# Summing the two up blocks of a seven-product unit with an accumulating DMA instead of a GpSimd subtraction

## The chip, the core and the metric

The kernel runs on one core of a Trainium2 chip. The metric is the device time of one launch in microseconds (us); the lower the better. Engines are called as in the profile: PE (TensorE matmul), PEld (its weight loads), DVE (VectorE), ACT (ScalarE), POOL (GpSimd), SP (SyncE, which issues the weight loads from HBM).

## The reference

One decoder layer over 256 tokens with a model width of 2048 in float32: a mixer (mLSTM and retention heads with one input and one output projection) and then a SwiGLU feed-forward network of width 5632, each between RMS norms. The change touches only the feed-forward part:

```
h = rmsnorm(x, g_ffn_pre)
ff = (silu(h @ w_gate) * (h @ w_up)) @ w_down
x = x + rmsnorm(ff, g_ffn_post)
```

## The kernel before

Every float32 weight is split into a rounded part and a rest (`w_hi` by ACT, `w_lo` by DVE as raw minus `w_hi`), so that a product is three fast matmuls. The weights arrive in `raw`, four chunks of 128 x 2048, loaded by SP's queue up to four units ahead; `w_hi` and `w_lo` have four slots each (AHEAD), and ACT may fill a slot only when PE has finished the piece that used it last.

A **unit** of the feed-forward part is two blocks of 128 weight rows by two blocks of 512 columns: for gate and up one block column of `w_up` and one of `w_gate`; for the down product two block columns of `w_down`. A plain unit (R) has two pieces, up and gate. A **seven-product unit** (S) computes the 2x2 block product with seven block products in place of eight, as Strassen and Winograd do, in four pieces, 0 to 3. A group of gate and up (512 columns, nine of them with the plan RRSRSRSR, then one RRSRSRRR) has its S units at n = 2, 4, 6, called the first, second and third unit below. The two halves of the down product have five S units each. That makes 29 + 10 = 39 S units.

In a unit's chunk the four blocks stand side by side: b12 and b22 (the up half), b11 and b21 (the gate half). Around the products three engines work on them:

- POOL, **T3** (L613): b12 becomes b22 - b12, as soon as the up half has arrived. In the down product five small token sums (L637 to L645) follow here.
- ACT hi0 and DVE lo0 round piece 0 (blocks b22 and b11). Then DVE, **T2** (L1559): b11 becomes b12 + b11. It waits for its own lo0 and for T3.
- ACT hi1 and DVE lo1 round piece 1 (b21).
- POOL, **T1** (L617): b22 becomes b22 - b11, after T2. POOL, **T4** (L619): b21 becomes b21 - b11, after lo1.
- ACT hi2 and DVE lo2 round piece 2 (b12 and b11; hi2 waits for T3 and T2). ACT hi3 and DVE lo3 round piece 3 (b22 and b21; hi3 waits for T1 and T4).

The hi's of S pieces are L983, of R pieces L972; the lo's are L1553 and L1550. Each engine executes its list in order. On DVE the order is lo0, T2, lo1, lo2, lo3, then the two lo's of the next R unit, then the next unit's lo0. On POOL it is T3 of a unit, T1, T4, then T3 of the next unit. PE waits for the lo of each piece (L1681 holds all its matmuls). SP reloads a chunk when the last lo that reads it is done.

The POOL part before, of which one unit is:

```
pool.wait_ge(raw_up[q], up_arrived(i, n))
pool.tensor_tensor(b12, b22, b12, ALU.subtract).then_inc(t3_ready, 1)
if between:
    between()
pool.wait_ge(t2_ready, made + 1)
pool.tensor_tensor(b22, b22, b11, ALU.subtract).then_inc(t14_ready, 1)
pool.wait_ge(lo_done, ff_base(i) + (plan.base[n] + 2))
pool.tensor_tensor(b21, b21, b11, ALU.subtract).then_inc(t14_ready, 1)
```

POOL's own queue carries four DMAs before the change: `neg_rows` (L591) and `neg_all` (L593) early, and the two post-norm gains (L606, L628), the last of them right ahead of the first T3 of the down product.

Of the kernel before, what the change touches and what calls it, by code (L numbers as in the profile page):

```python
# [24 lines left out]
ALU = mybir.AluOpType  # L25
# [28 lines left out]
FF_GROUPS = D_FF // 512  # L54
# [152 lines left out]
def hybrid_layer(nc, x, positions, g_mix_pre, w_in, conv_w, conv_b, b_igate, b_fgate, g_mlstm_head,  # L207
                 g_ret_head, w_out, g_mix_post, g_ffn_pre, w_gate, w_up, w_down, g_ffn_post,
                 inv_freq, out):
    with ExitStack() as ctx:  # L210
# [157 lines left out]
        s_ready = sem("s_ready")  # L368
        t3_ready = sem("t3_ready")
        t2_ready = sem("t2_ready")  # L370
        t14_ready = sem("t14_ready")
        p1_out = sem("p1_out")
        part_step = sem("part_step")
        part_done = sem("part_done")
# [195 lines left out]
        def _(pool):  # L570
# [37 lines left out]
            def weight_sums(i, n, plan, between=None):  # L608

                q, made = chunk_of(i, n), sums_index(i, n)  # L610
                b12, b22, b11, b21 = (raw[:, q, 512 * c:512 * (c + 1)] for c in range(4))
                pool.wait_ge(raw_up[q], up_arrived(i, n))
                pool.tensor_tensor(b12, b22, b12, ALU.subtract).then_inc(t3_ready, 1)  # L613
                if between:
                    between()
                pool.wait_ge(t2_ready, made + 1)
                pool.tensor_tensor(b22, b22, b11, ALU.subtract).then_inc(t14_ready, 1)  # L617
                pool.wait_ge(lo_done, ff_base(i) + (plan.base[n] + 2))
                pool.tensor_tensor(b21, b21, b11, ALU.subtract).then_inc(t14_ready, 1)  # L619

            with pool.Fori(1, FF_GROUPS - 1) as i:
                for n in SEVEN:
                    weight_sums(i, n, FULL)
            for n in SEVEN[:2]:
# [5 lines left out]
            def token_sums(d, n):  # L630

                a11, a21 = d_whole[:, 0, 0:P], d_whole[:, 0, P:SEQ]
                a12, a22 = d_whole[:, 1, 0:P], d_whole[:, 1, P:SEQ]
                if d:
                    pool.wait_ge(d_step, 5 * d)
                    pool.wait_ge(d_ready, d)
                pool.tensor_tensor(d_whole[:], ffT[:, 2 * n:2 * n + 2, 0:SEQ].bitcast(F32),  # L637
                                   ffT[:, 2 * n:2 * n + 2, SEQ:2 * SEQ].bitcast(F32), ALU.add).then_inc(d_step, 1)
                pool.wait_ge(d_step, 5 * d + 1)
                pool.tensor_tensor(d_sum[:, 0], a21, a22, ALU.add).then_inc(d_step, 1)  # L640
                pool.tensor_tensor(d_sum[:, 2], a11, a21, ALU.subtract).then_inc(d_step, 1)
                pool.wait_ge(d_step, 5 * d + 2)
                pool.tensor_tensor(d_sum[:, 1], d_sum[:, 0], a11, ALU.subtract).then_inc(d_step, 1)
                pool.wait_ge(d_step, 5 * d + 4)
                pool.tensor_tensor(d_sum[:, 3], a12, d_sum[:, 1], ALU.subtract).then_inc(d_step, 1)  # L645

# [8 lines left out]
        def _(act):  # L655
# [306 lines left out]
            def unit_hi(i, odd, plan, m):  # L962
# [12 lines left out]
                if piece == 0:  # L975
                    act.wait_ge(raw_up[q], arrived)
                    act.wait_ge(raw_full[q], arrived + 16 * (R_FF + 2))
                elif piece == 2:
                    act.wait_ge(t3_ready, sums_index(i, n) + 1)
                    act.wait_ge(t2_ready, sums_index(i, n) + 1)  # L980
                elif piece == 3:
                    act.wait_ge(t14_ready, 2 * sums_index(i, n) + 2)
                act.activation(slot_blocks(w_hi, slot, piece), seven_blocks(piece, q),  # L983
                               ACT.Copy).then_inc(hi_done, 1)

# [75 lines left out]
        def _(dve):  # L1061
# [426 lines left out]
            def up_sums(i, plan, c0, subs=None):  # L1488

                dve.wait_ge(part_done, 2 * i)  # L1490
                dve.wait_ge(sub_done, ff_base(i) + (subs or plan.subs - 1))
                for t in range(TT):
                    dve.tensor_tensor(ff(t, i), ff(t, i), bank[:, c0 + 2 + t, :], ALU.add).then_inc(up_sum, 1)

            def gate_sum_of(i, t, c0):

# [26 lines left out]
            def seven_sums(j):  # L1523

                k = 2 * SEVEN[j]
                whole = s_whole[:, j]
                a11, a21 = whole[:, 0, 0:P], whole[:, 0, P:SEQ]
                a12, a22 = whole[:, 1, 0:P], whole[:, 1, P:SEQ]
                link(dve.tensor_tensor(whole, h2T[:, k:k + 2, 0:SEQ].bitcast(F32),
                                       h2T[:, k:k + 2, SEQ:2 * SEQ].bitcast(F32), ALU.add))  # L1530
                link(dve.tensor_tensor(s_sum[:, j, 0], a21, a22, ALU.add))
                link(dve.tensor_tensor(s_sum[:, j, 1], s_sum[:, j, 0], a11, ALU.subtract))
                link(dve.tensor_tensor(s_sum[:, j, 2], a11, a21, ALU.subtract))
                dve.tensor_tensor(s_sum[:, j, 3], a12, s_sum[:, j, 1], ALU.subtract).then_inc(s_summed, 1)

# [8 lines left out]
            def unit_lo(i, odd, plan, m):  # L1544
# [10 lines left out]
                   .then_inc(lo_done, 1)  # L1555
                if piece == 0:
                    dve.wait_ge(lo_done, ff_base(i) + (m + 1))
                    dve.wait_ge(t3_ready, sums_index(i, n) + 1)
                    dve.tensor_tensor(raw[:, q, 1024:1536], raw[:, q, 0:512], raw[:, q, 1024:1536], ALU.add)\  # L1559
                       .then_inc(t2_ready, 1)  # L1560

            def partial_sums(i, plan, s0):
# [2 lines left out]
                p7, p5, p6 = bank[:, s0, :], bank[:, s0 + 1, :], bank[:, s0 + 3, :]  # L1565
                dve.wait_ge(sub_done, ff_base(i) + plan.after_seven)
                dve.wait_ge(p1_out, i)
                dve.tensor_tensor(u4, p1, p6, ALU.add).then_inc(part_step, 1)
                dve.wait_ge(part_step, 2 * i - 1)
                dve.tensor_tensor(u3, u4, p7, ALU.add).then_inc(part_step, 1)  # L1570
                dve.wait_ge(part_step, 2 * i)
# [526 lines left out]
```

## Time and profile before

| | |
|---|---|
| median of 3 runs | 1212.13 us (1212.02 to 1212.75) |
| profiled execution, its time | 1212.14 us |
| profiled execution, its span | 1210.4 us |
| mean granted TensorE clock | 0.998 of full speed (2.4 GHz) |
| busy: PE, PEld, DVE, ACT, POOL | 1193.8, 997.9, 926.5, 673.1, 265.7 us |
| DMA | 230.67 MB, 191 GB/s over the span |

The span runs from the first to the last instruction; the run's own time is 1.7 us more. The feed-forward groups with S units lie from about 520 us of the span on, the down product from 964 us to the end. A row of the timeline gives the start, the length, the engine, the line, the operation and its output and inputs; the bracket at its end is the idle time of that engine just before, and who ended it. A row with x2 or more merges instructions that follow on each other.

### The profile page before, as it was taken

The page shows a single profiled execution, that of the slowest core. Times are in us where ns is not written, and L with a number is a line of the kernel's source. Part 1 is how long each engine was busy: PE and PEld are TensorE (multiplying, and loading weights), DVE is VectorE, ACT ScalarE, POOL GpSimd, SP SyncE. Part 2 cuts the span into 40 slices and gives each one's busy share as a digit, 9 for nine tenths or more (in the row PEclk, how much of TensorE's full clock was granted, in tenths as well). Part 3 has the DMA queues.
Part 4 walks back from the last instruction along what each step waited for, and adds up shares of the span by engine and source line. Part 5 has one row for each costly group of instructions (what it writes and reads, how often), then busy time and mean ns, then how long its engine had stood idle before and what let it go on. Part 6 is the DMA issues. An engine that isn't in the chain of part 4 may idle for free.

```text
span 1210.4 us, 16331 instructions
## 1 busy us (share of the span) xinstructions
PE 1193.8 (99%) x5766; PEld 997.9 (82%) x5766; DVE 926.5 (77%) x1162; ACT 673.1 (56%) x890; POOL 265.7 (22%) x202
## 2 busy tenths in 40 slices
PE   8999999999999999999999999999999999999997
PEld 7888888888888888888888888888888878887885
DVE  6657777877777655777887888788888788669866
ACT  5654766474654645656555555555656555445543
POOL 1000200000000000004333323432332287227710
PEclk9999999999999999999999999999999999999999
DMA  8656868768686556454565556566555745764562
GB/s 312 206 154 159 230 168 174 170 135 219 161 198 194 194 189 199 158 199 154 195 209 208 190 187 214 172 208 208 196 188 188 255 156 199 243 193 158 188 225 70
DMA packets 122723, 230.67 MB, mean 191 GB/s; under 512 B 8104, under 2 KB 24752, under 8 KB 122032
## 3 DMA queue, kind: packets, MB, share of 16 engines
q1 hardware_dynamic: 122208, 226.85, 60.4%
q0 software_dynamic: 464, 3.15, 0.6%
q8 instruction: 30, 0.49, 0.2%
q14 instruction: 21, 0.17, 0.0%
HBM read 227.88 MB, written 2.11 MB: 190 GB/s over the span
## 4 chain that ended last, share of the span: by engine, by line
PE 93%; DVE 3%; ACT 2%; DMA 1%; issue 0%; SPq 0%; DVEq 0%; ACTq 0%
PE bank L1681 92%; DMA resid<-in_x 1%; PE bank L1958 1%; DVE w_lo L1553 1%; DVE w_lo L1074 0%; ACT w_hi L668 0%; PE bank L1686 0%; PE bank L1875 0%; DVE ff_out L1618 0%; ACT decay L778 0%; ACT w_hi L983 0%; ACT L824 0%; DVE w_lo L1550 0%; DVE h L1101 0%; DVE gT L1288 0%
## 5 line engine op out<-in xcount | busy, mean ns | idle before, releaser
L1681 PE MATMUL bank<-w_hi,h2T 128*128 128x512 f32 x1126 | 359.2, 390 | 0.0
L1074 DVE TENSOR_TENSOR w_lo<-raw,w_hi 128x1024 fp32r<-128x1024 f32 x172 | 209.3, 1222 | 127.6 <-ACT w_hi L668 126.9
L668 ACT ACTIVATE w_hi<-raw 128x1024 fp32r<-128x1024 f32 x172 | 180.9, 1058 | 174.3 <-PE bank L1681 155.1
L1681 PE MATMUL bank<-hT,w_hi 128*128 128x512 f32 x768 | 270.5, 396 | 0.0
L1553 DVE TENSOR_TENSOR w_lo<-raw,w_hi 128x1024 fp32r<-128x1024 f32 (+1 forms) x156 | 206.1, 1326 | 71.6 <-ACT w_hi L983 71.5
L1681 PEld LDWEIGHTS bank<-w_hi,h2T 128*128 128x128 f32 x1126 | 211.4, 188 | 44.0
L1550 DVE TENSOR_TENSOR w_lo<-raw,w_hi 128x1024 fp32r<-128x1024 f32 x170 | 213.3, 1287 | 34.7 <-ACT w_hi L972 34.1
L983 ACT ACTIVATE w_hi<-raw 128x1024 fp32r<-128x1024 f32 (+1 forms) x156 | 148.6, 954 | 159.7 <-PE bank L1681 133.1
L972 ACT ACTIVATE w_hi<-raw 128x1024 fp32r<-128x1024 f32 x170 | 174.6, 1055 | 89.1 <-PE bank L1681 88.8
L1681 PE MATMUL bank<-hT,w_lo 128*128 128x256 f32 x768 | 214.6, 279 | 0.0
L1681 PE MATMUL bank<-w_lo,h2T 128*128 128x512 f32 x543 | 211.3, 389 | 0.0
L1681 PE MATMUL bank<-w_hi,ffT 128*128 128x512 f32 x604 | 190.3, 390 | 0.3 <-DVE w_lo L1550 0.3
L1681 PEld LDWEIGHTS bank<-hT,w_hi 128*128 128x128 f32 x768 | 143.9, 187 | 31.6
L1681 PEld LDWEIGHTS bank<-hT,w_lo 128*128 128x128 f32 x768 | 145.0, 189 | 0.0
L1681 PEld LDWEIGHTS bank<-w_hi,ffT 128*128 128x128 f32 x604 | 113.4, 188 | 25.7 <-DVE w_lo L1550 2.1
L1681 PEld LDWEIGHTS bank<-w_lo,h2T 128*128 128x128 f32 x543 | 102.0, 188 | 21.0
L617 POOL TENSOR_TENSOR raw<-raw 128x512 f32<-128x512 f32 x39 | 62.2, 1595 | 252.4 <-DVE raw L1559 252.4
L1681 PE MATMUL bank<-w_lo,ffT 128*128 128x512 f32 x302 | 117.6, 389 | 0.0
L613 POOL TENSOR_TENSOR raw<-raw 128x512 f32<-128x512 f32 x39 | 63.6, 1630 | 226.7 <-DMA raw<-in_w_up 190.7
L1681 PE MATMUL bank<-w_hi,hT 128*128 128x512 f32 x256 | 81.3, 393 | 1.6 <-DVE w_lo L1074 1.6
L1681 PE MATMUL bank<-w_hi,mixT 128*128 128x512 f32 x256 | 80.1, 391 | 0.0
L1681 PEld LDWEIGHTS bank<-w_lo,ffT 128*128 128x128 f32 x302 | 56.7, 188 | 11.4
(232 smaller groups left out, 1300.7 us busy)
## 6 DMA issues: line engine op xcount, KB each, us to landing
raw<-in_w_in SPq DMA_DIRECT2D x63, 1024.0 KB, 10.5
raw<-in_w_down SPq DMA_DIRECT2D x88, 512.0 KB, 5.0
raw<-in_w_up SPq DMA_DIRECT2D x80, 512.0 KB, 4.0
raw<-in_w_gate SPq DMA_DIRECT2D x80, 512.0 KB, 4.9
raw<-in_w_out SPq DMA_DIRECT2D x16, 1024.0 KB, 5.0
raw<-in_w_gate SPq DMA_DIRECT2D x4, 1024.0 KB, 5.3
raw<-in_w_up SPq DMA_DIRECT2D x4, 1024.0 KB, 6.0
resid<-in_x SPq DMA_DIRECT2D x2, 1024.0 KB, 7.3
```

Source lines behind the costliest of these rows:

```text
L613: pool.tensor_tensor(b12, b22, b12, ALU.subtract).then_inc(t3_ready, 1)
L617: pool.tensor_tensor(b22, b22, b11, ALU.subtract).then_inc(t14_ready, 1)
L668: act.activation(part_of(w_hi, rnd, s), src, ACT.Copy).then_inc(hi_done, 1)
L972: act.activation(w_hi[:, slot, :], raw[:, q, SUB * piece:SUB * (piece + 1)], ACT.Copy).then_inc(hi_done, 1)
L983: act.activation(slot_blocks(w_hi, slot, piece), seven_blocks(piece, q), ACT.Copy).then_inc(hi_done, 1)
L1074: dve.tensor_tensor(part_of(w_lo, rnd, s), raw_sub(rnd, s)[1], part_of(w_hi, rnd, s).bitcast(F32), ALU.subtract).then_inc(lo_done, 1)
L1550: dve.tensor_tensor(w_lo[:, slot, :], raw[:, q, SUB * piece:SUB * (piece + 1)], w_hi[:, slot, :].bitcast(F32), ALU.subtract).then_inc(lo_d ...
L1553: dve.tensor_tensor(slot_blocks(w_lo, slot, piece), seven_blocks(piece, q), slot_blocks(w_hi, slot, piece).bitcast(F32), ALU.subtract)\
L1681: return pe.matmul(out_, lhsT, rhs, start=start, stop=stop, skip_group_check=True)
L1958: ins = pe.transpose(bank[:, b0 + j // 2, c:c + P], ff(t)[:, j * P:(j + 1) * P], ident)
```

## The change

T3 becomes a DMA that POOL issues and that adds b22 onto b12 in place; its semaphore goes up by 16 when the data has landed. As this is a sum and not a difference, signs turn: the token sums, T1 and T4, the product sums on DVE (same number of operations, of the same shapes). On POOL T4 now comes ahead of T1, and both stand behind the wait for lo1; T1 and T4 have a semaphore each. hi2 no longer waits for T3. POOL's loop over the groups is written out instead of run as a loop.

```diff
--- before.py
+++ after.py
@@ -368,7 +368,8 @@
         s_ready = sem("s_ready")
         t3_ready = sem("t3_ready")
         t2_ready = sem("t2_ready")
-        t14_ready = sem("t14_ready")
+        t1_ready = sem("t1_ready")
+        t4_ready = sem("t4_ready")
         p1_out = sem("p1_out")
         part_step = sem("part_step")
         part_done = sem("part_done")
@@ -610,15 +611,15 @@
                 q, made = chunk_of(i, n), sums_index(i, n)
                 b12, b22, b11, b21 = (raw[:, q, 512 * c:512 * (c + 1)] for c in range(4))
                 pool.wait_ge(raw_up[q], up_arrived(i, n))
-                pool.tensor_tensor(b12, b22, b12, ALU.subtract).then_inc(t3_ready, 1)
+                pool.dma_start(b12, b22, accum_op=ALU.add).then_inc(t3_ready, 16)
                 if between:
                     between()
+                pool.wait_ge(lo_done, ff_base(i) + (plan.base[n] + 2))
                 pool.wait_ge(t2_ready, made + 1)
-                pool.tensor_tensor(b22, b22, b11, ALU.subtract).then_inc(t14_ready, 1)
-                pool.wait_ge(lo_done, ff_base(i) + (plan.base[n] + 2))
-                pool.tensor_tensor(b21, b21, b11, ALU.subtract).then_inc(t14_ready, 1)
-
-            with pool.Fori(1, FF_GROUPS - 1) as i:
+                pool.tensor_tensor(b21, b21, b11, ALU.add).then_inc(t4_ready, 1)
+                pool.tensor_tensor(b22, b11, b22, ALU.subtract).then_inc(t1_ready, 1)
+
+            for i in range(1, FF_GROUPS - 1):
                 for n in SEVEN:
                     weight_sums(i, n, FULL)
             for n in SEVEN[:2]:
@@ -637,10 +638,10 @@
                 pool.tensor_tensor(d_whole[:], ffT[:, 2 * n:2 * n + 2, 0:SEQ].bitcast(F32),
                                    ffT[:, 2 * n:2 * n + 2, SEQ:2 * SEQ].bitcast(F32), ALU.add).then_inc(d_step, 1)
                 pool.wait_ge(d_step, 5 * d + 1)
-                pool.tensor_tensor(d_sum[:, 0], a21, a22, ALU.add).then_inc(d_step, 1)
+                pool.tensor_tensor(d_sum[:, 0], a22, a21, ALU.subtract).then_inc(d_step, 1)
                 pool.tensor_tensor(d_sum[:, 2], a11, a21, ALU.subtract).then_inc(d_step, 1)
                 pool.wait_ge(d_step, 5 * d + 2)
-                pool.tensor_tensor(d_sum[:, 1], d_sum[:, 0], a11, ALU.subtract).then_inc(d_step, 1)
+                pool.tensor_tensor(d_sum[:, 1], d_sum[:, 0], a11, ALU.add).then_inc(d_step, 1)
                 pool.wait_ge(d_step, 5 * d + 4)
                 pool.tensor_tensor(d_sum[:, 3], a12, d_sum[:, 1], ALU.subtract).then_inc(d_step, 1)
 
@@ -976,10 +977,10 @@
                     act.wait_ge(raw_up[q], arrived)
                     act.wait_ge(raw_full[q], arrived + 16 * (R_FF + 2))
                 elif piece == 2:
-                    act.wait_ge(t3_ready, sums_index(i, n) + 1)
                     act.wait_ge(t2_ready, sums_index(i, n) + 1)
                 elif piece == 3:
-                    act.wait_ge(t14_ready, 2 * sums_index(i, n) + 2)
+                    act.wait_ge(t1_ready, sums_index(i, n) + 1)
+                    act.wait_ge(t4_ready, sums_index(i, n) + 1)
                 act.activation(slot_blocks(w_hi, slot, piece), seven_blocks(piece, q),
                                ACT.Copy).then_inc(hi_done, 1)
 
@@ -1490,7 +1491,7 @@
                 dve.wait_ge(part_done, 2 * i)
                 dve.wait_ge(sub_done, ff_base(i) + (subs or plan.subs - 1))
                 for t in range(TT):
-                    dve.tensor_tensor(ff(t, i), ff(t, i), bank[:, c0 + 2 + t, :], ALU.add).then_inc(up_sum, 1)
+                    dve.tensor_tensor(ff(t, i), bank[:, c0 + 2 + t, :], ff(t, i), ALU.subtract).then_inc(up_sum, 1)
 
             def gate_sum_of(i, t, c0):
 
@@ -1528,8 +1529,8 @@
                 a12, a22 = whole[:, 1, 0:P], whole[:, 1, P:SEQ]
                 link(dve.tensor_tensor(whole, h2T[:, k:k + 2, 0:SEQ].bitcast(F32),
                                        h2T[:, k:k + 2, SEQ:2 * SEQ].bitcast(F32), ALU.add))
-                link(dve.tensor_tensor(s_sum[:, j, 0], a21, a22, ALU.add))
-                link(dve.tensor_tensor(s_sum[:, j, 1], s_sum[:, j, 0], a11, ALU.subtract))
+                link(dve.tensor_tensor(s_sum[:, j, 0], a22, a21, ALU.subtract))
+                link(dve.tensor_tensor(s_sum[:, j, 1], s_sum[:, j, 0], a11, ALU.add))
                 link(dve.tensor_tensor(s_sum[:, j, 2], a11, a21, ALU.subtract))
                 dve.tensor_tensor(s_sum[:, j, 3], a12, s_sum[:, j, 1], ALU.subtract).then_inc(s_summed, 1)
 
@@ -1555,7 +1556,7 @@
                    .then_inc(lo_done, 1)
                 if piece == 0:
                     dve.wait_ge(lo_done, ff_base(i) + (m + 1))
-                    dve.wait_ge(t3_ready, sums_index(i, n) + 1)
+                    dve.wait_ge(t3_ready, 16 * sums_index(i, n) + 16)
                     dve.tensor_tensor(raw[:, q, 1024:1536], raw[:, q, 0:512], raw[:, q, 1024:1536], ALU.add)\
                        .then_inc(t2_ready, 1)
 
@@ -1565,7 +1566,7 @@
                 p7, p5, p6 = bank[:, s0, :], bank[:, s0 + 1, :], bank[:, s0 + 3, :]
                 dve.wait_ge(sub_done, ff_base(i) + plan.after_seven)
                 dve.wait_ge(p1_out, i)
-                dve.tensor_tensor(u4, p1, p6, ALU.add).then_inc(part_step, 1)
+                dve.tensor_tensor(u4, p1, p6, ALU.subtract).then_inc(part_step, 1)
                 dve.wait_ge(part_step, 2 * i - 1)
                 dve.tensor_tensor(u3, u4, p7, ALU.add).then_inc(part_step, 1)
                 dve.wait_ge(part_step, 2 * i)
```

## Rows read from the trace of the kernel before

**Rows 1.** The page, chain that ended last: shares of the span by engine

```profile
PE 93%; DVE 3%; ACT 2%; DMA 1%; issue 0%; SPq 0%; DVEq 0%; ACTq 0%
```

**Rows 2.** Windows over the down product: length, then busy time of each engine

```profile
964.00:1073.00 109.00, 107.87 (x477) 87.76 (x476) 82.65 (x67) 57.01 (x62) 57.89 (x41) 1.00 0.61 207
1073.00:1180.00 107.00, 105.55 (x462) 85.73 (x461) 86.36 (x72) 55.34 (x64) 56.62 (x40) 1.00 0.56 190
```

**Rows 3.** Timeline, PE and PEld: first and last third-unit wait, and the longest

```profile
572.06 0.19 PEld L1681 LDWEIGHTS bank<-w_hi,s_third 128*128 128x128 f32 x1 [0.27 <-DVE w_lo L1553]
...
913.62 0.19 PEld L1681 LDWEIGHTS bank<-w_hi,s_third 128*128 128x128 f32 x1 [0.30 <-DVE w_lo L1553]
...
1098.69 0.50 PE L1681 MATMUL bank<-w_hi,d_ops 128*128 128x512 f32 x1 [1.16 <-DVE w_lo L1553]
```

**Rows 4.** Waits, the whole span: total us, times, longest

```profile
ACT w_hi L983 <- POOL raw L619: 25.4, 10, 2.6
```

**Rows 5.** Timeline of POOL, second and third unit of one gate/up group

```profile
718.62 1.29 POOL L613 TENSOR_TENSOR raw<-raw 128x512 f32<-128x512 f32 x1
726.42 1.68 POOL L617 TENSOR_TENSOR raw<-raw 128x512 f32<-128x512 f32 x1 [6.51 <-DVE raw L1559]
728.06 1.29 POOL L619 TENSOR_TENSOR raw<-raw 128x512 f32<-128x512 f32 x1
729.30 2.28 POOL L613 TENSOR_TENSOR raw<-raw 128x512 f32<-128x512 f32 x1
...
738.51 2.27 POOL L619 TENSOR_TENSOR raw<-raw 128x512 f32<-128x512 f32 x1
```

**Rows 6.** Timeline of DVE, the same stretch

```profile
718.94 3.19 DVE L1553 TENSOR_TENSOR w_lo<-raw,w_hi 128x1024 fp32r<-128x1024 f32 x2
722.05 2.35 DVE L1550 TENSOR_TENSOR w_lo<-raw,w_hi 128x1024 fp32r<-128x1024 f32 x2
...
726.26 0.68 DVE L1553 TENSOR_TENSOR w_lo<-raw,w_hi 128x512 fp32r<-128x512 f32 x1
728.24 2.20 DVE L1553 TENSOR_TENSOR w_lo<-raw,w_hi 128x1024 fp32r<-128x1024 f32 x1 [1.29 <-ACT w_hi L983]
730.91 1.76 DVE L1553 TENSOR_TENSOR w_lo<-raw,w_hi 128x1024 fp32r<-128x1024 f32 x1 [0.47 <-ACT w_hi L983]
...
736.11 0.69 DVE L1559 TENSOR_TENSOR raw<-raw 128x512 f32<-128x512 f32 x1
736.71 0.69 DVE L1553 TENSOR_TENSOR w_lo<-raw,w_hi 128x512 fp32r<-128x512 f32 x1
738.32 1.31 DVE L1553 TENSOR_TENSOR w_lo<-raw,w_hi 128x1024 fp32r<-128x1024 f32 x1 [0.92 <-ACT w_hi L983]
```

**Rows 7.** Timeline of ACT, the hi's of the R unit ahead of the second unit

```profile
720.89 2.01 ACT L972 ACTIVATE w_hi<-raw 128x1024 fp32r<-128x1024 f32 x2 [0.20 <-PE bank L1681]
```

**Rows 8.** Timeline of POOL and DVE, a second unit where DVE came first

```profile
642.75 2.35 POOL L619 TENSOR_TENSOR raw<-raw 128x512 f32<-128x512 f32 x1
...
642.72 1.23 DVE L1553 TENSOR_TENSOR w_lo<-raw,w_hi 128x1024 fp32r<-128x1024 f32 x1 [1.10 <-ACT w_hi L983]
```

**Rows 9.** DMA issues: timeline row of POOL; then KB each, us to landing

```profile
964.09 0.56 POOL L628 DMA_DIRECT2D g_post<-in_g_ffn_post  x1 [21.87 <-PE bank L1681]
...
raw<-in_w_up SPq DMA_DIRECT2D x80, 512.0 KB, 4.0
...
out<-resid SPq DMA_DIRECT2D x8, 256.0 KB, 2.5
...
g_post<-in_g_ffn_post POOLq DMA_DIRECT2D x1, 1024.0 KB, 6.4
...
neg_rows<-h POOLq DMA_DIRECT2D x1, 8.0 KB, 7.4
```

**Rows 10.** Timeline of POOL and DVE, one unit of the down product

```profile
1007.36 2.28 POOL L613 TENSOR_TENSOR raw<-raw 128x512 f32<-128x512 f32 x1
...
1009.94 2.04 DVE L1553 TENSOR_TENSOR w_lo<-raw,w_hi 128x1024 fp32r<-128x1024 f32 x1 [1.45 <-ACT w_hi L983]
```

## The prediction

> **What bounds the kernel now.** I read the chain that ended last first: PE makes 93% of it [rows 1], so any change of time must come as more or less waiting on PE. The timeline of PE and PEld from 520 us on, where the S units lie, then shows which waits there are. In the gate/up groups nearly all are one kind: nine weight loads ahead of a third unit's last piece wait 0.27 to 0.40 us each for lo3, 2.9 us in all [rows 3]. In the down product PE is short of its windows by 109.00 - 107.87 = 1.13 and 107.00 - 105.55 = 1.45 us, 2.58 us together, the largest piece being the 1.16 us ahead of one lo [rows 2, 3]. So some 5.5 us is all that the S units can give back, while a loss has no such bound.
>
> The list of waits says what stands behind lo3: ACT's hi3 waited ten times for T4, 25.4 us in all [rows 4]. The POOL and DVE timelines side by side show why T4 is late. An uncontended POOL operation takes 1.29 us, but T4 of the third unit takes 2.27: it came at 738.51 while DVE was in lo2 (738.32). The other way round, the second unit's lo2 takes 2.20 us instead of the 1.23 of another group [rows 8] since T4 had started 0.18 us before it [rows 5, 6]. Whoever comes first with two inputs in SBUF keeps the other out until it is through. T3 plays in this too: at 718.62 it delays the pair lo2, lo3 (3.19 us for two of 1.23), and at 729.30 it lies under lo2 and then lo3 (1.76 us) [rows 5, 6].
>
> **What goes away.** 39 subtractions on POOL. POOL is not the bound, so their time is worth nothing by itself; what counts is that DVE isn't kept out by T3.
> - Second unit: lo2 and lo3 lose about 0.7 us of waiting, but the next lo's (722.05) can't start before their hi's, at 720.89 + 2.01/2 = 721.90 [rows 6, 7]. So about 0.1 us of it reaches lo0, T2 and lo1.
> - Third unit: lo3 takes 1.23 in place of 1.76 us, and T2 and lo1 come 0.45 to 0.5 us earlier than 736.11 and 736.71 [rows 6].
>
> **What comes in.** A DMA issue on POOL: 0.56 us by the one for the gain [rows 9], less than the 1.29 it replaces. Then the landing, for which the trace has no accumulating transfer. The lower end is 2.5 us, a 256 KB store; the upper end 7.4 us, 8 KB on POOL's own queue; a 1 MB load on that queue took 6.4, a 512 KB load on SP's 4.0 [rows 9]. The sum reads 256 KB twice, so I take the 512 KB row: 4.0 us. What waits for it is T2 on DVE, and behind T2 in DVE's list lo1, lo2 and lo3, hence ACT's hi2 and hi3, hence PE; SP's next load of the chunk waits for lo3. From the place of T3 to T2 there are 725.65 - 718.62 = 7.0 us in the second unit (T2 being 0.61 ahead of lo1) and 736.11 - 729.30 = 6.8 us in the third [rows 5, 6]; first units have more. At 4.0 us the wait is covered. If the cover were gone, each microsecond above 6.7 would cost about one in the third unit and nearly one in the second.
>
> The Trainium skill (DMA: Bandwidth & Descriptors, Anatomy of one DMA) fits a GpSimd-queue DMA as 2.0 us plus its bytes over 436 GB/s, an estimate of 2.6 us for 256 KB, or 3.2 with the second read counted. The rows of POOL's queue, 6.4 us for 1 MB and 7.4 for 8 KB, are slower than the fit, which is why I don't go below 4.0; the sum would be the same by either, as both are covered.
>
> **What moves.** T4 and T1 change places, and both now stand behind lo1. Before, T1 started 0.16 us after lo1 began (726.42, 726.26) and then was kept out by it, so it took 1.68 us [rows 5, 6]. After, the first of the two starts some 0.08 us behind the end of lo1, with DVE idle, and takes 1.29. Its end moves from 728.10 to 726.26 + 0.68 + 0.08 + 1.29 = 728.31, less the 0.1 us gained above: 728.2. So the new wait costs 0.1 us, not 0.6. Behind POOL's wait stand T1 and the next DMA issue; the first has hi3 waiting for it.
>
> What then decides is **who comes first**, the second POOL operation or lo2. It follows the first by 1.25 us (728.06 to 729.30), so it starts at 728.27 - 0.1 = 728.17; lo2 starts when its hi is ready, at 728.24 [rows 5, 6]. I take POOL first, by 0.07 us. Then lo2 goes on as before, done at 730.4, and lo3, free of T3, ends 0.5 us earlier. In the third unit POOL's second operation would start at 736.71 + 0.69 + 0.08 + 1.25 - 0.45 = 738.28, against lo2 at 738.32. If it is first, hi3 starts about 1 us earlier and the wait of PE goes; if it is second, it ends where T4 ends now (738.51 + 2.27 = 740.78) and nothing is lost [rows 5, 6].
>
> **Edits at nothing.** The turned signs, the token sums and the product sums keep the number and shape of their operations. ACT has one wait less on hi2 and one more on hi3. The written-out loop sits under POOL's idle time (6.51 us ahead of T1 [rows 5]). The 39 transfers, 10 MB, add to 230 MB moved; weights come up to four units ahead and land in 4.0 us [rows 9], so a slower load is hidden.
>
> **The down product.** The token sums stand between T3 and T1 there, so the landing has more time. T3 (1007.36, 2.28 us) and the first token sum behind it keep lo3 to 2.04 us [rows 10]; with an issue of 0.56 us POOL is done sooner and lo3 should end 0.5 us earlier. Two waits stay: T3 of the first down unit is queued behind the 1 MB gain, which lands only after 6.4 us [rows 9], and the long one at 1098.69 has other work around it as well.
>
> **The sum.** Gate/up: PEld runs ahead of the matmuls, so of 2.9 us of weight-load waits I count half, -1.45 us (bounds 0 and -2.9). Down: half of 2.58 us, -1.3 us (0 to -2.6). From 1212.14, the profiled execution's own time, which is the median within 0.01: 1212.14 - 2.75 = 1209.4 us, with 1207.0 to 1211.8 as this case's own range.
>
> **Rivals.**
> - **DVE comes first (slower).** Place: lo2 of the second unit. A group of before shows it: lo2 at 642.72, POOL at 642.75 with 2.35 us instead of 1.29, ending 2.38 us after lo2 began [rows 8]. Then POOL's second operation of the second unit ends at 728.24 + 2.38 = 730.62, where T4 ended at 729.35. hi3 follows it and lo3 after another 1.09 us, at 731.7 to 732.9, against 730.91 + 1.76 = 732.67 now: 0.3 us late. The third unit's T2 inherits that, its first POOL operation lasts until 739.0, lo2 goes next, and the last one ends at 739.0 + 2.38 = 741.4 in place of 740.78. That is +0.6 us on PE in each of nine groups, 5.4 us, less 1.3 in the down product: 1216.2 us. It decides where POOL's start passes lo2's, 0.07 us away; a POOL wait that costs more than 0.08 us is enough. For it: the margin. Against it: in most groups of before lo2 lost by 0.18 us.
> - **The sum lands late.** It decides at a landing over 6.7 us. At 7.4 [rows 9] T2 of the second unit is about 0.7 us late and passes it on to the next issue, so the third is 1.4 us late: 9 x 1.4 = 12.6, less 1.3, gives 1223.4 us. For it: the two slow rows of POOL's queue. Against: both of those touch HBM, and the first is the queue's first use.
>  The Trainium skill (SBUF — State Buffer, Who interferes with whom) has a rule on this side: a DMA of GpSimd's queue is starved of descriptors while DVE runs an operation that holds both shared ports; it infers that a tensor_tensor doesn't, and no row of this case shows a POOL issue under one.
> - **Nothing comes out of it.** POOL's issue takes as long as the subtraction, or the order of POOL and DVE falls out differently from group to group: 1211 to 1213 us, 1212.1 as the middle. Then the change doesn't do what it says for PE: POOL is relieved, and no wait of PE ends sooner.
>
> **How the numbers follow.** Forecast 0.45, DVE first 0.27, late landing 0.15, nothing 0.13. A measurement can tell about 0.2% here, 2.4 us. The forecast's middle lies just beyond that: 0.32 of its 0.45 faster, 0.13 the same. DVE first: 0.23 slower, 0.04 the same. Late: 0.12 slower, 0.03 the same. Nothing: 0.11 the same, 0.02 faster. Together 0.34 faster, 0.31 the same, 0.35 slower. The range takes in the forecast from 1207.0 and DVE first up to 1218.0; most of the late landing stays outside.
>
> **What would show it.** Right: POOL has DMA rows of about 0.6 us in place of L613, landing by 4 to 5 us; T2 never waits for a DMA; lo2 of second units keeps 2.2 us; hi3 waits for POOL less than 25.4 us; the third-unit waits of PE shrink. Wrong: second-unit lo2 at 1.2 us with POOL at 2.3 beside it, or DVE rows of T2 that wait for a DMA, and PE waits for lo3 of over 0.4 us in every group.

## The result, and the profile after

The changed kernel takes 1216.16 us in the median (1214.53 to 1221.68), the kernel before in the same sessions 1212.01 us: a ratio of 1.0036, 95% interval 1.0026 to 1.0045. It is slower by 0.36%. The forecast, 1209.4 us, had the wrong sign; the time lies in the range, and 0.04 us from the rival "DVE comes first", priced at 1216.2 us.

The page of the changed kernel: the chain that ended last by engine, the change's lines on POOL, and the median landing of its DMA (the time from its issue until its data is there).

```profile
PE 84%; DVE 6%; DMA 4%; issue 2%; ACT 2%; POOL 1%; SPq 0%; DVEq 0%; ACTq 0%; POOLq 0%
...
L614 POOL DMA_DIRECT2D raw<-raw x39 | 33.7, 863 | 226.4 <-DMA raw<-in_w_up 191.7
...
L620 POOL TENSOR_TENSOR raw<-raw 128x512 f32<-128x512 f32 x39 | 70.3, 1803 | 0.0
...
raw<-raw POOLq DMA_DIRECT2D x39, 256.0 KB, 3.3
```

PE's share of the chain fell from 93% [rows 1] to 84%: there are more waits in it. The issue takes 0.86 us, not 0.56, and the sum lands after 3.3 us in the median, not 4.0. L620 is T1, now the second of the two POOL operations: 1.80 us on average, so many of its instances are held up.

The median hides two kinds of landing. Below are the shortest, median and longest of the 39; then one first unit, issued at 577.87, with the windows over its landing and over that of the next unit (length, busy time of each engine, then clock, share of the DMA engines and GB/s):

```profile
DMA to landing us min/median/max: 3.2/3.3/9.5
...
raw<-raw POOLq DMA_DIRECT2D x1, 256.0 KB, 6.5
...
577.87:584.39 6.52, 6.52 (x30) 5.39 (x29) 6.49 (x10) 2.96 (x4) 0.87 (x1) 1.00 0.98 287
591.76:595.00 3.24, 3.24 (x16) 2.69 (x15) 2.67 (x4) 2.35 (x4) 0.85 (x2) 1.00 0.47 81
```

In the first units of nine groups weight loads keep the DMA engines busy at the same time (0.98 here), and T3 lands after 4.8 to 6.5 us. In the second and third units it lands after 3.2 to 3.4 us. T2 comes about 10 us after the issue in those first units, 6.7 us or more in second ones and 5.9 or more in third ones, so each landing but one is covered. That the weight loads make these landings long is likely and was not tested.

The list of waits of the changed kernel (us in total, times, longest), which answers to [rows 3, 4], and the two lines of before for PEld and PE:

```profile
ACT w_hi L984 <- POOL raw L620: 31.2, 12, 3.3
PEld bank L1682 <- DVE w_lo L1554: 15.0, 22, 3.1
PE bank L1682 <- DVE w_lo L1554: 6.6, 11, 2.7
DVE raw L1560 <- DMA raw<-raw: 3.2, 1, 3.2
...
PEld bank L1681 <- DVE w_lo L1553: 8.7, 19, 1.6
PE bank L1681 <- DVE w_lo L1553: 2.3, 3, 1.2
```

ACT's hi3 waits more for POOL (25.4 us before [rows 4]), and PEld and PE wait for a lo twenty-two and eleven times, where it was nineteen and three before. DVE waited for the new DMA just once.

Second unit of the group of [rows 5, 6]: POOL, then DVE, then PEld and PE, by start and duration.

```profile
729.72 1.28 POOL L619 TENSOR_TENSOR raw<-raw 128x512 f32<-128x512 f32 x1 [7.25 <-DVE w_lo L1554]
730.97 2.29 POOL L620 TENSOR_TENSOR raw<-raw 128x512 f32<-128x512 f32 x1
...
728.94 0.68 DVE L1554 TENSOR_TENSOR w_lo<-raw,w_hi 128x512 fp32r<-128x512 f32 x1
730.88 1.23 DVE L1554 TENSOR_TENSOR w_lo<-raw,w_hi 128x1024 fp32r<-128x1024 f32 x1 [1.26 <-ACT w_hi L984]
734.44 1.23 DVE L1554 TENSOR_TENSOR w_lo<-raw,w_hi 128x1024 fp32r<-128x1024 f32 x1 [2.33 <-ACT w_hi L984]
...
735.72 0.19 PEld L1682 LDWEIGHTS bank<-w_hi,s_hi 128*128 128x128 f32 x1 [0.35 <-DVE w_lo L1554]
746.59 0.50 PE L1682 MATMUL bank<-w_hi,s_third 128*128 128x512 f32 x1 [0.38 <-DVE w_lo L1554]
```

lo2 starts at 730.88 and T1 at 730.97: DVE is first by 0.09 us, lo2 takes its plain 1.23 us, T1 takes 2.29. hi3 waits for T1, and lo3 comes 2.33 us after lo2 is through. Before, POOL was first by 0.18 us, T4 took 1.29 and lo2 2.20 [rows 5, 6]. PE now waits for weights of the second unit as well as of the third.

What that costs can be read from the pace of the groups. The first partial sum that DVE makes behind each third unit (L1568 before, L1569 after) marks it. Kernel before: the first row, two neighbours, the ninth and the tenth; then the same ends of the changed kernel.

```profile
575.33 0.68 DVE L1568 TENSOR_TENSOR part<-part,bank 128x512 f32<-128x512 f32 x1
617.94 0.68 DVE L1568 TENSOR_TENSOR part<-part,bank 128x512 f32<-128x512 f32 x1
661.24 0.68 DVE L1568 TENSOR_TENSOR part<-part,bank 128x512 f32<-128x512 f32 x1
916.89 0.68 DVE L1568 TENSOR_TENSOR part<-part,bank 128x512 f32<-128x512 f32 x1
957.90 0.68 DVE L1568 TENSOR_TENSOR part<-part,bank 128x512 f32<-128x512 f32 x1
```

```profile
576.74 0.68 DVE L1569 TENSOR_TENSOR part<-part,bank 128x512 f32<-128x512 f32 x1
922.99 0.68 DVE L1569 TENSOR_TENSOR part<-part,bank 128x512 f32<-128x512 f32 x1
964.16 0.68 DVE L1569 TENSOR_TENSOR part<-part,bank 128x512 f32<-128x512 f32 x1
```

(922.99 - 576.74) / 8 = 43.28 us a group after, (916.89 - 575.33) / 8 = 42.70 before: +0.58 us a group on average. The group from 617.94 to 661.24 is the one of [rows 8], in which DVE came first: it took 43.30 us where the others of before took 42.61. The case that now holds in the second unit of every group could be priced from the trace of before. From the tenth mark to the end of the span the down product takes 1216.9 - 964.16 = 252.7 us against 1210.4 - 957.90 = 252.5: no gain there in this execution. The profiled execution's own time, 1218.65 us, is 2.5 above the median; 1.5 of it lies ahead of the first mark (a later run, whose code is the same up to the down product, is there at 575.21), so groups are compared by their pace and not by their place. By the medians the down product comes out a little better: of the 4.15 us that the change costs, (964.16 - 576.74) - (957.90 - 575.33) = 4.85 lie between the first and the tenth mark, which leaves -0.7 for it, an estimate.

The first unit of the down product after the change: POOL's queue, T2 on DVE, and PE.

```profile
970.35 0.60 POOL L629 DMA_DIRECT2D g_post<-in_g_ffn_post  x1 [20.78 <-PE bank L1682]
970.95 0.89 POOL L614 DMA_DIRECT2D raw<-raw  x1
...
980.55 0.69 DVE L1560 TENSOR_TENSOR raw<-raw 128x512 f32<-128x512 f32 x1 [3.16 <-DMA raw<-raw]
...
989.16 0.50 PE L1682 MATMUL bank<-w_hi,d_ops 128*128 128x512 f32 x1 [2.66 <-DVE w_lo L1554]
```

T3 was issued right behind the 1 MB gain on the same queue and landed after 9.5 us, the longest of 39 (3.0 us more than any other). Weight loads were under way as well: the DMA engines were 0.97 busy until then. T2 waited 3.16 us for it and PE 2.66 us a little later, in one place more than all 2.58 us that PE was short of in the down product before [rows 2].

### The profile page after: what moved, and what is told of

Its sections match the earlier page's. It is cut to its first block, busy times and chain, and to the rows that moved or that the text cites. A ratio compares the mean times of both kernels' runs of the same rounds, so it can differ in the third digit from the quotient of the medians.

```text
span 1216.9 us, 16281 instructions
## 1 busy us (share of the span) xinstructions
PE 1195.6 (98%) x5766; PEld 998.3 (82%) x5766; DVE 893.6 (73%) x1162; ACT 670.9 (55%) x890; POOL 231.9 (19%) x202
## 4 chain that ended last, share of the span: by engine, by line
PE 84%; DVE 6%; DMA 4%; issue 2%; ACT 2%; POOL 1%; SPq 0%; DVEq 0%; ACTq 0%; POOLq 0%
PE bank L1682 83%; DMA raw<-in_w_in 2%; DVE w_lo L1554 2%; DVE w_lo L1075 1%; ACT w_hi L984 1%; DMA raw<-raw 1%; DMA resid<-in_x 1%; POOL raw L620 1%; PE bank L1959 1%; DVE w_lo L1551 0%; POOL raw L619 0%; ACT w_hi L669 0%; DVE gT L1299 0%; PE bank L1687 0%; PE bank L1876 0%
## 5 line engine op out<-in xcount | busy, mean ns | idle before, releaser
L1554 DVE TENSOR_TENSOR w_lo<-raw,w_hi 128x1024 fp32r<-128x1024 f32 (+1 forms) x156 | 180.3, 1155 | 102.7 <-ACT w_hi L984 102.3
L614 POOL DMA_DIRECT2D raw<-raw x39 | 33.7, 863 | 226.4 <-DMA raw<-in_w_up 191.7
L620 POOL TENSOR_TENSOR raw<-raw 128x512 f32<-128x512 f32 x39 | 70.3, 1803 | 0.0
```

The lines of the kernel that those rows point to most:

```text
L614: pool.dma_start(b12, b22, accum_op=ALU.add).then_inc(t3_ready, 16)
L620: pool.tensor_tensor(b22, b11, b22, ALU.subtract).then_inc(t1_ready, 1)
L1554: dve.tensor_tensor(slot_blocks(w_lo, slot, piece), seven_blocks(piece, q), slot_blocks(w_hi, slot, piece).bitcast(F32), ALU.subtract)\
```

## The experiments

The theories. **A**: the loss in the gate/up groups comes from the order on POOL: with both operations behind lo1, lo2 comes ahead of the second. **B**, the rival: it comes from the DMA itself, its issue, its landing or its port. **C**: a separate loss at the start of the down product, from T3's place in the queue behind the gain.

The table has the median, the ratio to the runs of before beside it, the mean length of a gate/up group (from the first mark to the ninth, over 8) and the stretch from the tenth mark to the end of the span, all in us. Before and after are worked out above, the others from the same rows of their traces.

| kernel | median | ratio, 95% interval | a group | down stretch |
|---|---|---|---|---|
| before | 1212.01 | | 42.70 | 252.5 |
| the change | 1216.16 | 1.0036 [1.0026, 1.0045] | 43.28 | 252.7 |
| e1: old order, DMA | 1206.98 | 0.9961 [0.9947, 0.9974] | 42.39 | 249.7 |
| e2: change, gain behind T3 | 1214.03 | 1.0021 [1.0011, 1.0030] | 43.28 | 249.2 |
| e3: change, lo2 waits for T4 | 1207.58 | 0.9964 [0.9951, 0.9978] | 42.39 | 250.4 |
| e4: new order, no DMA | 1219.65 | 1.0066 [1.0052, 1.0080] | 43.51 | 252.9 |
| e5: e1 and e2 | 1206.07 | 0.9955 [0.9938, 0.9972] | 42.39 | 248.8 |
| e6: e3 and e2 | 1206.51 | 0.9958 [0.9943, 0.9973] | 42.39 | 249.3 |
| e7: e1, extra subtraction | 1224.99 | 1.0111 [1.0092, 1.0130] | 44.20 | 250.2 |
| e8: e1, extra memsets | 1207.57 | 0.9960 [0.9944, 0.9975] | 42.39 | 250.3 |
| e9: e7, lo2 waits for T1 | 1214.85 | 1.0022 [1.0007, 1.0036] | 43.07 | 250.2 |
| e10: before, lo2 waits for T1 | 1210.08 | 0.9986 [0.9973, 0.9999] | 42.39 | 252.9 |

### e1: the DMA with the old order

```
                 pool.wait_ge(t2_ready, made + 1)
+                pool.tensor_tensor(b22, b11, b22, ALU.subtract).then_inc(t1_ready, 1)
+                pool.wait_ge(lo_done, ff_base(i) + (plan.base[n] + 2))
                 pool.tensor_tensor(b21, b21, b11, ALU.add).then_inc(t4_ready, 1)
-                pool.tensor_tensor(b22, b11, b22, ALU.subtract).then_inc(t1_ready, 1)
```

The first wait for `lo_done`, ahead of these lines, goes as well.

> The changed kernel with the old order of POOL's two operations: T1 right behind T2, then the wait for lo1, then T4; T3 stays a DMA. Theory A (the loss in gate/up comes from POOL's second operation arriving at the shared reads just after lo2, because both operations now stand behind lo1): T4 starts before lo2 again, the group period falls from 43.3 us to 42.6 or less, and the time from 1216.2 to 1209.5 to 1211. The wait for the first T3 of the down product stays. Theory B (the DMA itself costs the time: its longer issue of 0.86 us, its landing, or its load on the DMA engines): the period stays at 43.3 us and the time at 1215 to 1217.

1206.98 us: faster than before by 0.39% and than the change by 0.75%. The second operations, T4, of the second and third unit, and the two lo2:

```profile
727.15 1.28 POOL L620 TENSOR_TENSOR raw<-raw 128x512 f32<-128x512 f32 x1
737.34 1.29 POOL L620 TENSOR_TENSOR raw<-raw 128x512 f32<-128x512 f32 x1
...
727.28 2.23 DVE L1554 TENSOR_TENSOR w_lo<-raw,w_hi 128x1024 fp32r<-128x1024 f32 x1 [1.26 <-ACT w_hi L984]
737.40 2.30 DVE L1554 TENSOR_TENSOR w_lo<-raw,w_hi 128x1024 fp32r<-128x1024 f32 x1 [1.18 <-ACT w_hi L984]
```

POOL is first by 0.13 and 0.06 us, in the third unit too, where it was last before. PE waits nowhere between the first and the tenth mark, so 42.39 us is the length of a group without such waits, and no version can show less there by ending waits. The DMA is the same as in the change, so B falls for these groups, and A stands. T2 still waits once for the DMA, 1.4 us, in the first down unit.

### e2: the change, with the gain's DMA behind the first down T3

```
-            pool.wait_ge(sub_done, DOWN_FIRST)
-            pool.dma_start(g_post2[:], ...).then_inc(post_in, 16)
...
             def token_sums(d, n):
+                if not d:
+                    pool.wait_ge(sub_done, DOWN_FIRST)
+                    pool.dma_start(g_post2[:], ...).then_inc(post_in, 16)
+                    pool.wait_ge(ff_lo, 2 * FF_GROUPS - 2)
...
-            pool.wait_ge(ff_lo, 2 * FF_GROUPS - 2)
```

The two waits, for PE (`sub_done`) and for the last lo's (`ff_lo`), go behind T3 together with the gain's issue. So the edit does two things: T3 has no 1 MB load ahead of it, and it is issued earlier.

> The changed kernel with one move: the 1 MB gain load on POOL's queue is issued behind the first T3 of the down product and not ahead of it. Theory C (that T3 lands late, 9.5 us after its issue, only because it is queued behind the gain; this costs PE about 3 us once): T2 no longer waits 3.2 us for the DMA, the 2.66 us wait of PE near 989 us goes, and the time is 1212.5 to 1214; the gate/up period stays at 43.3 us. Against C (late for the landing's own sake, or the wait is covered): 1215.5 to 1216.5 and T2 waits as before.

1214.03 us, 2.1 below the change; T2 waits for no DMA, and the 2.66 us wait is gone. A group keeps its 43.28 us. So T3's place behind the gain is a second loss beside the order. The intervals of the two ratios overlap a little, so this rests on the medians and on the waits that are gone. The issue of the first down T3 and its landing:

```profile
963.35 0.88 POOL L614 DMA_DIRECT2D raw<-raw  x1 [15.24 <-DMA raw<-in_w_down]
...
raw<-raw POOLq DMA_DIRECT2D x1, 256.0 KB, 4.7
```

It is issued 0.7 us behind the tenth mark, where the change issued it 6.8 us behind, and lands after 4.7 us. The edit alone doesn't part the earlier issue from the free queue. The traces speak for the queue: with the gain right ahead, the change, e1, e3, e7, e8 and e9 show landings of 7 to 9.5 us, and with the gain behind, e2, e5 and e6 show 4.7 to 6.4. At 6.5 us, the longest of the other units, T3 would have landed by 977.5 in the change, when T2 was ready (980.55 - 3.16 = 977.39). So C holds for the extra landing; why it is still over 3.3 us with the gain behind, with weight loads under way, stays open. In the two profiled executions the down stretch differs by 3.5 us, more than the medians do: the late landing need not cost the same in every execution.

### e3: the change, with lo2 held back until T4 is through

```
                 dve.wait_ge(hi_done, ff_base(i) + (m + 1))
+                if plan.units[n] == "S" and piece == 2 and down_half(i) is None:
+                    dve.wait_ge(t4_ready, sums_index(i, n) + 1)
```

> The changed kernel with one more wait: in gate/up units DVE's lo2 waits until POOL's first operation (T4) is done, so that T1, which follows on POOL without a wait, always comes to the shared reads before lo2. Order of T4 and T1, DMA and all else as changed. Theory A: T1 takes 1.29 us in place of 2.29, lo2 lengthens to some 2.3 us, hi3 no longer waits for POOL, the period falls to 42.6 us or less and the time to 1209.5 to 1211. Theory B: an added wait on DVE can only cost; 1216 or more.

1207.58 us. The order on POOL is that of the change, and one wait on DVE takes 8.6 us off. T1 and lo2 of the second unit:

```profile
727.06 1.28 POOL L620 TENSOR_TENSOR raw<-raw 128x512 f32<-128x512 f32 x1
...
727.12 2.30 DVE L1556 TENSOR_TENSOR w_lo<-raw,w_hi 128x1024 fp32r<-128x1024 f32 x1 [1.41 <-POOL raw L619]
```

lo2 starts 0.06 us behind T1, T1 takes 1.28 us, and a group 42.39. In the gate/up groups it is not where T1 and T4 stand that costs, but which of the two starts first, lo2 or POOL's second operation.

### e4: the new order alone, T3 a subtraction as before

```
+                pool.wait_ge(lo_done, ff_base(i) + (plan.base[n] + 2))
                 pool.wait_ge(t2_ready, made + 1)
-                pool.tensor_tensor(b22, b22, b11, ALU.subtract).then_inc(t14_ready, 1)
-                pool.wait_ge(lo_done, ff_base(i) + (plan.base[n] + 2))
                 pool.tensor_tensor(b21, b21, b11, ALU.subtract).then_inc(t14_ready, 1)
+                pool.tensor_tensor(b22, b22, b11, ALU.subtract).then_inc(t14_ready, 1)
```

> The kernel before (T3 a POOL subtraction) with only the new order: POOL waits for lo1 and T2, then T4, then T1. Theory A: the order alone makes the loss; second-unit lo2 comes first, the period is 43.2 to 43.5 us and the time 1216 to 1219, more than the changed kernel's gate/up part since T3 still keeps DVE out. Theory B: 1211.5 to 1213, as before.

1219.65 us, a little over what A gave. POOL, DVE and the wait that follows from them:

```profile
731.82 2.27 POOL L619 TENSOR_TENSOR raw<-raw 128x512 f32<-128x512 f32 x1
...
731.49 1.46 DVE L1553 TENSOR_TENSOR w_lo<-raw,w_hi 128x1024 fp32r<-128x1024 f32 x1 [1.08 <-ACT w_hi L983]
...
ACT w_hi L983 <- POOL raw L619: 49.1, 18, 2.9
```

Here lo2 is ahead by 0.33 us. Against the runs of before beside them, the order alone costs 0.66%, the DMA with the old order gains 0.39%; the change has both and loses 0.36%, some of it by C.

### e5 and e6: both remedies

e5 is e1 and e2 together, e6 is e3 and e2.

> The order of before with the DMA, and the gain's issue behind the first down T3. If the two parts of the loss are separate (the order in the gate/up groups; POOL's queue at the start of the down product), their gains add: the 1.4 us for which T2 still waits for the DMA once goes, and with it most of the waits of 0.40 and 0.57 us on PE near 976 us: 1205.5 to 1206.7 us, against 1206.98 for the order alone. If that wait is covered by other work of PE, the time stays at 1207 within 0.5.

> POOL held first by a wait of DVE, and the gain's issue behind the first down T3: the down product then starts without the 9.5 us landing, which cost 2.1 us when it was taken out alone. If the parts add: 1205.5 to 1206.7 us from 1207.58. If the down product's own order (T4 before T1, with no wait of DVE there) costs by itself, it stays above 1207 with waits of 0.3 us and more in the down units.

1206.07 and 1206.51 us, the two fastest: 0.45 and 0.42% below before. Both stand about 1 us below the run without e2's edit (1206.98, 1207.58), as expected; their intervals overlap, so this step rests on the medians and on the down stretch, 248.8 against 249.7 and 249.3 against 250.4. e5 has the lowest median, with the DMA, the old order and no additional wait. But its order in the third units hangs on a lead of POOL of some 0.06 us, as in e1, and e7 below shows it flip; e6 settles it by a wait, for 0.4 us more in the median, within the intervals. The windows over e5's down product, laid as in [rows 2] from the tenth mark, which is 2.70 us earlier:

```profile
961.30:1070.30 109.00, 108.80 (x485) 89.63 (x484) 78.29 (x68) 57.46 (x62) 50.86 (x42) 1.00 0.66 220
1070.30:1177.30 107.00, 106.67 (x470) 87.89 (x469) 81.20 (x73) 56.87 (x66) 47.15 (x39) 1.00 0.62 199
```

PE is short of its windows by 0.20 and 0.33 us in place of 1.13 and 1.45. That is 2.05 us less idle, while the stretch is 3.7 us shorter: in windows of the same length PE does 485 and 470 matmuls instead of 477 and 462 [rows 2].

### e7 and e8: what T3's reads cost

e1, and behind T3's issue in each gate/up unit one more POOL operation into a scratch tile that nobody reads: a subtraction of two inputs in SBUF (e7), or two memsets, 128x1024 and 128x400, that take about as long in all (e8).

```
                 pool.dma_start(b12, b22, accum_op=ALU.add).then_inc(t3_ready, 16)
+                if i < FF_GROUPS - 1:
+                    pool.tensor_tensor(scratch[:, 0, :], resid[:, 0, 0:512], resid[:, 1, 0:512], ALU.subtract)...
```

Left out here are a semaphore that keeps the writes to the scratch tile apart, and the edit that puts POOL's two operations back in e1's order.

> The order of before with the DMA (1206.98 us), and on POOL, behind T3's issue in each gate/up unit, a subtraction of two inputs of T3's size into a scratch tile that nobody reads. Theory R (what the DMA saves is that T3's two reads no longer keep DVE's lo's out): the subtraction lies where T3 lay, takes 1.3 to 2.3 us, lengthens a lo of DVE to 1.7 us or more, and the waits of 0.27 to 0.40 us on PE come back: 1210 to 1212.5 us, a group's period of 42.6 us in place of 42.4. Theory P (it is POOL's time or its queue that counts): the same. Theory E (the gain comes from elsewhere, as the first down unit or the landing): 1207 within 0.6.

> The same place as in the run with the extra subtraction, but two memsets that read nothing, some 1.3 us of POOL in all. Theory R (the reads): DVE's lo's keep 1.23 us and the time stays at 1207 within 0.6. Theory P (POOL's time): 1210 to 1212.5 us like the subtraction. If memsets too lengthen DVE's operations, it comes between, and the rows of DVE say so.

1224.99 us with the reads and 1207.57 without. Theory P (POOL's time) falls for the gate/up groups: the memsets take 1.25 and 0.43 us and cost nothing that can be told, and a lo that runs beside one keeps its 1.23 us:

```profile
720.39 1.25 POOL L618 MEMSET two_tiles<- 128x1024 f32 x1
...
720.57 1.23 DVE L1560 TENSOR_TENSOR w_lo<-raw,w_hi 128x1024 fp32r<-128x1024 f32 x1
```

Theory R had the direction right and the size wrong, 1225 where I expected 1212.5 at most. e7's rows of POOL and DVE tell why:

```profile
726.68 1.68 POOL L618 TENSOR_TENSOR two_tiles<-resid 128x512 f32<-128x512 f32 x1
735.40 2.28 POOL L624 TENSOR_TENSOR raw<-raw 128x512 f32<-128x512 f32 x1
...
727.67 1.78 DVE L1558 TENSOR_TENSOR w_lo<-raw,w_hi 128x1024 fp32r<-128x1024 f32 x1 [0.46 <-ACT w_hi L988]
735.23 1.30 DVE L1558 TENSOR_TENSOR w_lo<-raw,w_hi 128x1024 fp32r<-128x1024 f32 x1 [0.94 <-ACT w_hi L988]
```

The subtraction stands behind an issue of 0.86 us, so it lies over lo3 (1.78 us at 727.67), everything behind lo3 shifts, and in the next unit lo2 comes 0.17 us ahead of T4 (735.23 and 735.40), which then takes 2.28 us. The order had flipped again.

### e9: e7 with lo2 held back until T1 is through

> The run with the extra subtraction (1224.99 us, a group's period of 44.20 us on average), with one more wait: lo2 of an S unit starts only when T1 is through, so that T4, which follows T1 at once, has the reads to itself. Theory 1 (half of that run's loss is the reads themselves, half that lo2 came 0.17 us before T4): T4 takes 1.3 us, the loss shrinks to 1210 to 1216 us. Theory 2 (the reads alone): it stays at 1222 us or above, with PE waiting behind T2 and lo1 rather than lo3.

e3's edit, with `t1_ready` in place of `t4_ready`, put on e7. 1214.85 us: of the 18.0 us that the subtraction cost, 10.1 went with the order and 7.9 stay. T4 takes 1.29 us in the stretch shown for e7, and a group 43.07 us. Reads that lie over a lo do cost here, but the larger part was who came first.

### e10: the kernel before with lo2 held back until T1 is through

> The kernel before, whose T3 is a subtraction, with the same wait: lo2 only after T1, so that no group has lo2 ahead of T4. Theory 1 (the DMA is worth 4 us by its own, as it takes T3's reads away): little comes of the wait, 1210 to 1212 us, a period of 42.6 us and the waits of PE behind lo3 as they were. Theory 2 (what the kernel with the old order and the DMA gained is only that the order is settled): 1207 to 1208 us without any DMA. In a third way (T3's reads under lo3 leave the wait no room) it gets slower, to 1213 us or more.

Same edit as e3, with `t14_ready` at one more than twice the unit's index. 1210.08 us, 0.14% below before, at the edge of what can be told. Neither theory held as a whole. Of theory 1 the time is right, of theory 2 what happened in the groups: they take 42.39 us, just as with the DMA, though T3's reads are back (the first row is T3, the second T4 of the third unit, the last its lo2).

```profile
727.85 2.29 POOL L613 TENSOR_TENSOR raw<-raw 128x512 f32<-128x512 f32 x1
737.06 1.28 POOL L619 TENSOR_TENSOR raw<-raw 128x512 f32<-128x512 f32 x1
...
737.13 2.30 DVE L1555 TENSOR_TENSOR w_lo<-raw,w_hi 128x1024 fp32r<-128x1024 f32 x1 [1.19 <-POOL raw L617]
```

So in the gate/up groups the DMA is worth only what the settled order is worth (in e1 it brings that order about by itself), and its own worth lies in the down product: 252.9 us there in e10, 249.7 in e1, 248.8 in e5. The medians say the same: e5 is 4.0 us below e10. What the DMA does in the down product can be seen on lo3, which T3 kept to 2.04 us before [rows 10]; the same unit in e1:

```profile
991.88 1.32 DVE L1554 TENSOR_TENSOR w_lo<-raw,w_hi 128x1024 fp32r<-128x1024 f32 x1 [1.45 <-ACT w_hi L984]
```

Whether it is T3's reads or POOL's time that counts there is not shown: e7 and e8 add their operations in gate/up units alone.

## Why the prediction was wrong

**The step that failed** is in "What moves": the second POOL operation "starts at 728.27 - 0.1 = 728.17; lo2 starts when its hi is ready, at 728.24 [...] I take POOL first, by 0.07 us". Measured, lo2 was first by 0.09. The 0.16 us between forecast and measurement can be laid out against hi2, which stands on ACT's timeline in both kernels and waits for PE there (before, then after, with the pair of lo's of the R unit ahead of T2):

```profile
727.14 1.06 ACT L983 ACTIVATE w_hi<-raw 128x1024 fp32r<-128x1024 f32 x1 [2.22 <-PE bank L1681]
```

```profile
724.69 2.36 DVE L1551 TENSOR_TENSOR w_lo<-raw,w_hi 128x1024 fp32r<-128x1024 f32 x2
...
729.79 1.06 ACT L984 ACTIVATE w_hi<-raw 128x1024 fp32r<-128x1024 f32 x1 [2.16 <-PE bank L1682]
```

- The 0.1 us of lead that I let T3's absence pass on to lo1 did not come. lo1 began 727.14 - 726.26 = 0.88 us ahead of hi2 before [rows 6] and 729.79 - 728.94 = 0.85 after. I had let it grow to 0.98: 0.13 us too much. The pair of lo's ahead of T2 starts 729.79 - 724.69 = 5.10 us ahead of hi2 after, and 727.14 - 722.05 = 5.09 before [rows 6]: the time that T3 no longer took didn't reach it. I had seen that its own hi's bound it [rows 7], and credited the lead above them.
- POOL started 0.10 us behind lo1's end (728.94 + 0.68 = 729.62, to 729.72), where I took 0.08: 0.02 us.
- lo2 followed hi2 by 1.09 us instead of 1.10: 0.01 us.

None of the three could be had to that precision: the lead of POOL in second units of before is 0.15 to 0.18 us in nine groups and -0.03 in the one of [rows 8]. The sign was set on a margin smaller than its own error, and the chances should have been near even between the two cases; I gave 0.45 against 0.27.

**The mechanism** was named, and rightly: whoever comes first keeps the other out until it is through. The Trainium skill says so too (SBUF — State Buffer, Who interferes with whom): issue order, not the shape of the operation, decides who blocks, and a VectorE operation with both inputs in SBUF contends with GpSimd's reads, not with an operation that only writes. This case's rows agree: T1 took 2.29 us where it started 0.09 us behind lo2 (the change) and 1.28 where it started 0.06 ahead (e3), and the subtraction of e7 cost 18.0 us where the memsets of e8 cost nothing that can be told.

**The rival's price** was good for a group: I put +0.6 us on each of nine, and a group has +0.58. But from the first to the tenth mark these make 4.85 us, not 5.4, and the down product has +0.2 in the profile, -0.7 by the medians, not -1.3. That the sum came within 0.04 us is luck: the two errors cancel.

**What goes away.** T3's reads were to give the gate/up groups 1.45 us. With the order settled and T3 kept (e10), a group is as short as with the DMA; with that order T3's reads cost PE nothing in these groups. The gain is 42.70 - 42.39 = 0.31 us a group, some 2.5 us over the eight (0.45 of it is lost again between the ninth and the tenth mark), and comes from T4 ahead of lo2 in the third units and in the one group of [rows 8].

**What comes in.** Right: the landing is covered, but for one unit, and the issue's 0.86 us stays under other work. The cover in third units is 6.0 us in most groups, not 6.8, and the landing has no single size: 3.3 us by the median, 4.8 to 6.5 in nine first units, which the prediction didn't tell apart. It also says that no row shows a POOL issue under a DVE operation with two inputs in SBUF. In the trace of the change 14 of the 39 issues lie under one almost wholly, and take 0.84 to 0.88 us, as the others do. The sentence on the Trainium skill's fit (DMA: Bandwidth & Descriptors, Anatomy of one DMA) gave an estimate of 2.6 us, or 3.2 with the second read counted; the measured median is 3.3, so the second estimate was nearer than the 512 KB row that I took; for those first units both are too low.

**The down product.** "Two waits stay: T3 of the first down unit is queued behind the 1 MB gain" saw the place and missed the size: I kept it as it was, and T3's landing there took 9.5 us, which with its later issue cost 2.1 us in the medians (e2). That is the late landing of the second rival, 6.7 us and over, in one unit of 39. The other wait that was to stay, 1.16 us at 1098.69, did not: the longest wait of PE in that second half is 0.32 us in e1 and 0.33 in e5. Apart from it, the term was undersized: not -1.3 us but -2.8 in e1 and -3.7 in e5. I had bounded it by PE's idle time, and e5's windows show that the idle time isn't all: before, PE got through fewer matmuls in the time that counts as busy (939 in 213.42 us, against 955 in 215.47), as far as the counts of the windows can be trusted (some records of matmuls can be missing). That late weight loads slow it there is likely and not shown.

**Edits at nothing.** Nothing speaks against them in the gate/up groups: e3 and e1 keep the turned signs, the token sums and the written-out loop, and have no wait of PE between the first and the tenth mark.

## What to carry to other kernels

Where two engines compete for the same reads and the one that starts first keeps them for its whole operation, a margin of 0.1 us between their starts is a branch, not a term: look for a group in which it already falls the other way and price the change by that group's length (43.30 against 42.61 us here), or settle it by a wait, which cost PE nothing here and gave 8.6 us. Put an operation that a third engine waits for on the winning side. And when a step becomes a DMA, read the queue that it joins: a transfer that was harmless ahead of a subtraction had a DMA behind it that landed after 7 to 9.5 us, against 4.7 to 6.4 with the two exchanged.

## What was not expected of the hardware

The accumulating DMA of 256 KB within SBUF keeps POOL for 0.86 us at its issue, where the plain load of the gain takes 0.60, and lands after 3.3 us by the median, 3.2 at the least. Beside weight loads that filled the DMA engines it took 4.8 to 6.5 us, and right behind a 1 MB load of the same queue, with weight loads too, 9.5. And POOL's writes didn't disturb DVE's reads: 1.7 us of memsets a unit moved nothing that can be told (e8), while a subtraction of the same length cost 18 us, 10 of them by turning the order (e9).
